# Attention sums with V as a 64-column stationary operand in two column tiles, bias and row maximum in one instruction

## What is computed

```python
def dilated_branch(q, k, v, rel_bias, window, dil):
    ...
    s = jnp.einsum("brnqhd,brnkhd->brnhqk", qb, kk) * (dh ** -0.5)
    ...
    s = s + bias.transpose(2, 0, 1)
    ...
    m = jnp.max(s, axis=-1, keepdims=True)
    p = jnp.exp(s - m)
    den = jnp.sum(p, axis=-1)
    o = jnp.einsum("brnqhk,brnkhd->brnqhd", p, vv) / den.transpose(0, 1, 2, 4, 3)[..., None]
    lse = (m[..., 0] + jnp.log(den)).transpose(0, 1, 2, 4, 3)
```

## Time and profile before

| | us |
|---|---|
| median of 3 runs (2899.11 to 2900.86) | 2900.39 |
| the profiled execution | 2887.13 |
| span of its trace | 2885.3 |
| attention, first to last matmul | 1396.5 to 1750.9 |

### The profile page before, as it was taken

One profiled execution on the slowest core, in us unless ns is written; L12 is line 12 of the kernel. 1 busy time (PEld: TensorE's weight loads), 2 busy tenths in 40 slices (PEclk: granted clock), 3 DMA queues, 4 the chain that ended last, 5 costly groups with the idle time before them and its releaser, 6 DMA issues. The chain is left out here.

```text
span 2885.3 us, 32536 instructions
## 1 busy us (share of the span) xinstructions
PE 2404.3 (83%) x9386; PEld 1351.9 (47%) x9387; DVE 1138.8 (39%) x1853; ACT 840.7 (29%) x1981; POOL 312.8 (11%) x298
## 2 busy tenths in 40 slices
PE   5779998898968999796799995999609999998940
PEld 2245554333424554685477773555404444444410
DVE  0122211666722263353478874565431111111126
ACT  3011111333223331121377784444101111111125
POOL 0000000000001110132113330000040000000022
PEclk9989999999988999898799997999859999999975
DMA  8631101111114664695222333444107756588778
GB/s 327 220 122 65 58 33 34 44 44 44 58 44 149 194 196 147 211 290 176 103 92 90 96 101 113 147 158 157 52 33 288 284 204 227 190 295 301 267 283 327
DMA packets 183271, 451.62 MB, mean 157 GB/s; under 512 B 42352, under 2 KB 78448, under 8 KB 169632
## 3 DMA queue, kind: packets, MB, share of 16 engines
q1 hardware_dynamic: 149200, 335.37, 34.3%
q10 hardware_dynamic: 21168, 72.36, 6.3%
q0 software_dynamic: 12832, 43.02, 4.3%
HBM read 321.22 MB, written 129.45 MB: 156 GB/s over the span
## 5 line engine op out<-in xcount | busy, mean ns | idle before, releaser
L1964 PE MATMUL ps<-ex_wgu,ex_xt 128*128 x800 | 355.3, 597 | 22.6 <-DMA ex_wgu<-in_w_gate_up 21.9
L418 PE MATMUL ps<-ht,pc_w 128*128 128x512 f32 x768 | 343.9, 610 | 33.9 <-ACT pc_pre L451 26.1
L334 PE MATMUL ps<-pt_wt,pt_ht 128*128 128x512 f32 (+1 forms) x768 | 250.7, 482 | 11.6 <-ACT pt_ht L344 11.5
L418 PEld LDWEIGHTS ps<-ht,pc_w 128*128 128x128 f32 x768 | 149.7, 196 | 227.3 <-issue 195.1
L1964 PEld LDWEIGHTS ps<-ex_wgu,ex_xt 128*128 128x128 f32 x800 | 148.9, 191 | 195.0 <-issue 195.0
L753 PE MATMUL ps<-ht,ci_w 128*128 128x512 f32 x512 | 224.5, 596 | 3.1 <-DMA ci_w<-in_w_chan 3.1
L1547 PE MATMUL ps<-w_out,mo_yt 128*128 128x512 f32 x512 | 224.4, 596 | 0.0
L334 PEld LDWEIGHTS ps<-pt_wt,pt_ht 128*128 128x128 f32 x768 | 127.0, 191 | 136.7 <-issue 123.0
L1360 PE MATMUL ps<-at_v,at_pt 128*128 128x128 f32 (+1 forms) x1200 | 184.0, 291 | 5.8 <-DMA at_v<-v_d 5.8
L1974 PE MATMUL ps<-ex_wd,ex_hidt 128*128 x400 | 181.8, 598 | 3.6 <-issue 2.2
L1422 ACT ACTIVATE at_p<-at_p,at_low 128x256 f32<-128x256 f32 (+1 forms) x384 | 174.0, 456 | 20.0 <-DVE at_low L1389 19.6
(11 more groups left out here) (288 smaller groups left out, 3112.6 us busy)
## 6 DMA issues: line engine op xcount, KB each, us to landing
ex_wgu<-in_w_gate_up SPq DMA_DIRECT2D x32, 2048.0 KB
ex_wd<-in_w_down SPq DMA_DIRECT2D x32, 1024.0 KB, 8.1
ys_d<-ex_y ACTq DMA_DIRECT2D x50, 512.0 KB
ada_w<-in_w_ada SPq DMA_DIRECT2D x12, 2048.0 KB, 8.5
at_v<-v_d SPq DMA_DIRECT2D x27, 512.0 KB, 4.0
o_d<-at_o SPq DMA_DIRECT2D x48, 264.0 KB
mo_o<-o_d SPq DMA_DIRECT2D x16, 792.0 KB, 8.8
ch_d<-pc_cv SPq DMA_DIRECT2D x12, 1024.0 KB, 3.9
```

Of the source, the lines that this page charges most:

```text
L334: last = nc.tensor.matmul(ps[:, bank, 0:hi - lo], ht[:, b, k, :], wt[:, k, lo:hi], start=(k == 0), stop=(k == KD - 1))
L418: last = nc.tensor.matmul(ps[:, g, :], w[:, b, k, :], m.ht[:, k, g * BANK:(g + 1) * BANK], start=(k == 0), stop=(k == KD - 1))
L1964: last = nc.tensor.matmul(ps[:, 2 + b, :], xt[:, b, k, :], wgu[:, bass.ds(half * WGU + k * 2 * DE, 2 * DE)], start=(k == 0), stop=(k == KD ...
```

## The change

The sums change roles. V, 64 columns of one head, becomes the stationary operand, and the transposed probabilities (128 columns) the moving one. The two heads of a step go to the two halves of the array's columns, and so to the two halves of the partitions of the result, which is now the sums transposed. At the end of a unit VectorE copies this (512 columns) to a new tile `ot`; TensorE turns it back with four transposes (`turn_o`, in the first step of the unit after next in the program's list, behind that step's `sums`); and VectorE copies it again into `o` in the second step (`take_o`). A last `turn_o` and `take_o` follow the last unit.

Scale, bias and maximum become one instruction for each head, `tensor_tensor_reduce`, which writes minus the scaled sum and its minimum. The bias table is multiplied by 8 to suit (one operation swapped for another in `bias_tables`), and `exp` gets a scale of -1. The copies of the transposed probabilities are shared: VectorE takes those of steps 1 and 3, ScalarE those of steps 0 and 2. The copy of `low` moves from VectorE to GpSimd, behind a wait for the last `exp` of the unit before.

```diff
@@ bias_tables
-                    nc.vector.tensor_tensor(rows[:, s], ps[0:AH, n, 0:BIAS_W], off[:, s], ALU.add).then_inc(*rows_ready.inc)
+                    nc.vector.scalar_tensor_tensor(rows[:, s], ps[0:AH, n, 0:BIAS_W], DH ** 0.5, off[:, s], ALU.mult, ALU.add).then_inc(*rows_ready.inc)
@@ attention
+        ot = R.sb("ot", [P, AW])
...
+        def take_pt(eng, copy, unit, s):
+            b, n, n2 = numbers(unit)
+            e, c, k = s % 2, n2 + s // 2, first_key(unit) // P
+            eng.wait_ge(*pt_done[e].n(c + 1))
+            eng.wait_ge(*pv_done[e].n(c))
+            copy(pt[:, e, :, k:, :], ps[:, 4 + e, :].rearrange("p (h k n) -> p h k n", h=2, k=2)[:, :, k:, :]).then_inc(*pt_ready[e].inc)
...
@@ SP
                         sp.wait_ge(*o_ready[b].n(n + 1))
+                        sp.wait_ge(*low_kept[b].n(n + 1))
@@ GpSimd, behind the gathers of q and k
+                    if prev:
+                        b, n, n2 = numbers(prev)
+
+                        pool.wait_ge(*p_ready[1].n(n2 + 2))
+                        pool.wait_ge(*out[b].n(n))
+                        pool.sem_inc(seen_pool, 1)
+                        nc.gpsimd.tensor_copy(o[:, b, AW:], low[:, b, :]).then_inc(*low_kept[b].inc)
@@ TensorE, sums
-                    for h in range(2):
-                        for k in range(k0, 2):
+                    for k in range(k0, 2):
+                        for h in range(2):
                             at = 2 * s + h
-                            w = slice(at * DH, min(at + 2, AH) * DH)
-                            last = nc.tensor.matmul(ps[:, 6 + b, w], pt[:, e, h, k, :], v[:, b, k, w], start=(k == k0), stop=(k == 1))
+                            last = nc.tensor.matmul(ps[h * DH:(h + 1) * DH, 6 + b, s * P:(s + 1) * P], v[:, b, k, at * DH:(at + 1) * DH], pt[:, e, h, k, :], start=(k == k0), stop=(k == 1))
                     last.then_inc(*pv_done[e].inc)
+                def turn_o(b, n):
+
+                    pe.wait_ge(*ot_ready[b].n(n))
+                    for s in range(STEPS):
+                        last = nc.tensor.transpose(ps[:, 6 + b, s * P:(s + 1) * P], ot[:, s * P:(s + 1) * P], m.ident)
+                    last.then_inc(*turned[b].inc)
...
                         if prev:
                             sums(prev, s)
+                        if s == 0 and earlier(unit, prev):
+                            turn_o(*earlier(unit, prev))
...
+                turn_o(numbers(prev)[0], UNITS // 2)
@@ VectorE
+                def take_o(b, n):
+                    dve.wait_ge(*turned[b].n(n))
+                    dve.wait_ge(*out[b].n(n - 1))
+                    nc.vector.tensor_copy(o[:, b, 0:AW], ps[:, 6 + b, :]).then_inc(*o_ready[b].inc)
+
                 for unit, prev in units(dve):
-                    if unit:
...
+                    for s in range(STEPS):
+                        if prev and s in (0, 2):
+                            take_pt(dve, nc.vector.tensor_copy, prev, s + 1)
+                        if unit:
...
+                            if s == 0:
+                                dve.wait_ge(*low_kept[b].n(n))
                             dve.wait_ge(*s_done[e].n(c + 1))
                             dve.wait_ge(*pt_done[e].n(c - 1))
-                            nc.vector.scalar_tensor_tensor(p[:, s, :, lo:], ps[:, 2 * e:2 * e + 2, lo:2 * P], DH ** -0.5, m.bias[:, unit[0][1], 2 * s:2 * s + 2, lo:], ALU.mult, ALU.add).then_inc(*s_read[e].inc)
-                            dve.wait_ge(*s_read[e].n(c + 1))
-                            nc.vector.tensor_reduce(low[:, b, 2 * s:2 * s + 2], p[:, s, :, lo:], AX.X, ALU.max, negate=True).then_inc(*max_ready[e].inc)
+                            dve.sem_inc(seen_dve, 1)
+                            for h in range(2):
+                                at = 2 * s + h
+                                nc.vector.tensor_tensor_reduce(p[:, s, h, lo:], ps[:, 2 * e + h, lo:2 * P], m.bias[:, unit[0][1], at, lo:], -(DH ** -0.5), BIG, ALU.add, ALU.min, stats(b, at)).then_inc(s_read[e].inc[0], 1)
+                        if s == 1 and earlier(unit, prev):
+                            take_o(*earlier(unit, prev))
                     if prev:
                         b, n, n2 = numbers(prev)
                         dve.wait_ge(*pv_done[1].n(n2 + 2))
-                        dve.wait_ge(*p_ready[1].n(n2 + 2))
-                        dve.wait_ge(*out[b].n(n))
-                        nc.vector.tensor_copy(o[:, b, AW:], low[:, b, :])
-                        nc.vector.tensor_copy(o[:, b, 0:AW], ps[:, 6 + b, :]).then_inc(*o_ready[b].inc)
+                        dve.wait_ge(*turned[1 - b].n(n + b))
+                        nc.vector.tensor_copy(ot[:, :], ps[:, 6 + b, :]).then_inc(*ot_ready[b].inc)
+                take_o(numbers(prev)[0], UNITS // 2)
@@ ScalarE
-                        if s >= 2 and unit:
-                            take_pt(unit, s - 2)
-                        elif s < 2 and prev:
-                            take_pt(prev, s + 2)
+                        if s == 3 and unit:
+                            take_pt(act, nc.scalar.copy, unit, 0)
+                        elif s == 1 and prev:
+                            take_pt(act, nc.scalar.copy, prev, 2)
...
-                                ins = nc.scalar.activation(p[:, s, h, lo:], p[:, s, h, lo:], ACT.Exp, bias=low[:, b, at:at + 1], accum_out=low[:, b, at + AH:at + AH + 1])
+                                ins = nc.scalar.activation(p[:, s, h, lo:], p[:, s, h, lo:], ACT.Exp, bias=low[:, b, at:at + 1], scale=-1.0, accum_out=low[:, b, at + AH:at + AH + 1])
```

More of the change, by code:

```diff
@@ L1270, in place @@
         return branch, BR[branch][0], first(i, j)
+    BIG = 3.0e38
     with Room(nc, "at") as R:
@@ L1284, in attention, with earlier @@
         q_ready, k_ready, o_ready = R.sigs("q_ready"), R.sigs("k_ready"), R.sigs("o_ready")
-        s_done, s_read, max_ready, p_ready = R.sigs("s_done", credit=3), R.sigs("s_read"), R.sigs("max_ready"), R.sigs("p_ready")
+        ot_ready, turned, low_kept = R.sigs("ot_ready"), R.sigs("turned"), R.sigs("low_kept")
+        seen_dve, seen_pool = R.plain("seen_dve"), R.plain("seen_pool")
+        s_done, s_read, p_ready = R.sigs("s_done", credit=3), R.sigs("s_read", step=2), R.sigs("p_ready")
         pt_done, pt_ready, pv_done = R.sigs("pt_done", credit=2), R.sigs("pt_ready"), R.sigs("pv_done", credit=3)
+        def earlier(unit, prev):
+            if unit:
+                b, n, _ = numbers(unit)
+                return None if isinstance(n, int) and n == 0 else (b, n)
+            return 1 - numbers(prev)[0], UNITS // 2
+        def take_pt(eng, copy, unit, s):
[4 more added lines that the diff above has]
+            copy(pt[:, e, :, k:, :], ps[:, 4 + e, :].rearrange("p (h k n) -> p h k n", h=2, k=2)[:, :, k:, :]).then_inc(*pt_ready[e].inc)
         with R.block() as block:
@@ L1373, in _, with stats @@
                             sums(prev, s)
+                        if s == 0 and earlier(unit, prev):
+                            turn_o(*earlier(unit, prev))
                     if not prev:
                         turn_p(unit, 0)
+                turn_o(numbers(prev)[0], UNITS // 2)
             @block.vector
             def _(dve):
-                for unit, prev in units(dve):
-                    if unit:
-                        b, n, n2 = numbers(unit)
-                        lo = first_key(unit)
-                        for s in range(STEPS):
+                def stats(b, at):
+                    return low[:, b, at:at + 1]
@@ new lines, in take_o @@
+                def take_o(b, n):
+                    dve.wait_ge(*turned[b].n(n))
+                    dve.wait_ge(*out[b].n(n - 1))
+                    nc.vector.tensor_copy(o[:, b, 0:AW], ps[:, 6 + b, :]).then_inc(*o_ready[b].inc)
+                for unit, prev in units(dve):
+                    for s in range(STEPS):
+                        if prev and s in (0, 2):
+                            take_pt(dve, nc.vector.tensor_copy, prev, s + 1)
+                        if unit:
+                            b, n, n2 = numbers(unit)
+                            lo = first_key(unit)
```

2 lines of the change are left out of this document (1 added, 1 removed).

## The result

The changed kernel is slower, by 1.7 to 2.3%: 2957.22 us median (2949.62 to 2963.15, 4 runs) against 2899.75 (2894.67 to 2900.86, 4 runs) of the kernel before, a ratio of 1.020 with a 95% interval of 1.0167 to 1.0233. The profiled execution took 2949.62 (span 2947.8), 62 more than that of the kernel before. Attention alone, from its first scores to the last of its sums, went from 354.1 to 406.8 us, so 53 of the difference lie there. Nearly all the rest lies ahead of it: attention starts 7.4 us later (at 1404.0), and the phase before it already starts 8.1 later (1378.9 against 1370.8). The same shows in e2_before_late_o, which alters nothing ahead of attention (1405.6), so I don't count it as the change's.

What follows compares the result with a forecast made beforehand. TensorE was taken to bound attention; full units -21.6 to -16.2 us, half units +2.5 to +6.7, end +1.5 and stalls +1 were taken as -12 from the 2900.4 median, giving 2888.5, range 2880 to 2936.

Steps and rivals of the forecast that it cites:

- the wait of SP: SP's extra wait for GpSimd's small copy, 2 to 3 us before the sums are there, costs nothing.
- the gain of the steps: TensorE's attention steps: 0.26 to 0.31 us saved per full step, 0.03 to 0.08 per half step, before turning back.
- slower: Outcome of a measurably slower kernel, resting on A, D and most of B and Rival E; chance 0.32.
- Rival E: Idle array time in half units drops attention's clock; each 20 us stretch costs about 9: 2898 to 2916; chance 0.06.
- A: Sums' column tiles run one behind the other, streams as long as today: +66 us, 2954; chance 0.12.
- B: Sums' column tiles run together but their loads don't hide: +20 to +45 us, 2908 to 2933; chance 0.11.
- third switch: A further change of array shape in each TensorE attention step, between sums and transposes, costing about 0.20 us.
- Turning back: Four transposes of the sums added to each unit on TensorE, without a further switch: 0.44 us.
- The end's 1.5 us: Attention's end: copy, four transposes and another copy after the last sums, 1.5 us more, not hidden.
- 1 us of stalls: Allowance for `turn_o` waiting on `ot` in half units, 0 to 0.3 us each; 1 us taken in all.
- C: `turn_o` waits for `ot`, or GpSimd's gathers come late, 0.1 to 0.3 us a unit: 2893 to 2903; chance 0.10.
- D: VectorE becomes the bound through a slower new instruction: +36 us, 2924; chance 0.07.

Runs made afterwards that it cites:

- e2_before_late_o: Kernel before, with only VectorE's copy of the 512 sums into o moved behind step 1 of the next unit; median 2948.65 us, ratio 1.0199.
- e1: Changed kernel with only SP's program altered: it stores the result of unit u-2 instead of u-1; median 2868.31 us, ratio 0.9901.
- e4: e1 with the sums' matmuls reordered in full units, both key blocks of one head first; median 2873.38 us, ratio 0.9927.
- e5: e1 with all copies of transposed probabilities on ScalarE, fused instruction kept on VectorE; median 2866.11 us, ratio 0.9908.
- e6: Changed kernel with the sums of before, no turning back, o copied at the unit's end; fusion and shared copies stay; median 2888.32 us, ratio 0.9978.
- e3: e1 with the fusion undone: scale and bias in one instruction, maximum in a second; copies stay shared; median 2893.55 us, ratio 0.9997.
- e8: e1 with the fusion undone and all copies of transposed probabilities on ScalarE; median 2873.39 us, ratio 0.9935.

## Why the prediction was wrong

I forecast 2888.5 (2880 to 2936), the median was 2957.2. Two terms failed: the wait of SP, put at nothing, and the gain of the steps, put too low. Point by point:

**SP's queue is the step that failed.** I wrote of SP's extra wait that it is for GpSimd's copy, "2 to 3 us before the sums are there. Cost nothing". Instead TensorE waited 54.7 us for V, 49 more than before. I looked at the wait that the diff adds and not at the one that it leaves in place: `o_ready` now comes half a unit or more later, and the next load of V is queued behind it. Its price could have been read from the trace of before: the store was issued right at the unit's end and the load 0.6 behind it, 3.6 us ahead of its sums, with a landing of 2.8, so there was 0.8 us to spare in a half unit. A delay of over two steps of 1.2 us had to break that. e2 shows that this alone makes 1.0199, e1 that its removal turns 1.020 into 0.9901. None of my rivals names this wait, so the 0.32 that I gave to "slower" stood on other causes.

**Rival E, the clock,** had the right effect and the wrong cause. I gave it 0.06 for the shapes. In e1, e4, e5 and e6 and in the kernel before the clock is at 1.00 (2.4 GHz) from attention's slow start (over by 1432) to its last sums, with old and with new shapes. The two kernels with waits for V show 0.50 (1.2 GHz): from 1697 to 1741 and again from about 1798 in the changed one, and for 27 us from 1777 in e2, besides short falls behind single pauses. In the changed kernel each fall began at a pause of 1.5 to 2.1 us or at most 1.5 us behind it. But it did not follow every such pause: eight of 1.35 to 1.74 us stand between 1745 and 1795, at 1.00 throughout. The shorter pauses in e3 and e8 (up to 1.0 us in e3 and 0.6 in e8) came with 1.00 throughout, behind the slow start. In the changed kernel five half units in a row took 8.7 us each, against 6.7 with the pause and 5.1 without. The runs of the changed kernel have a mean clock of 0.903 to 0.910 and are the longer the lower it is (2949.62 at 0.910, 2963.15 at 0.903). That the pauses bring the fall is what the pairs before and e2, and e1 and after, say: each differs in the pauses and not in the shapes. Why it fell where it did stays open.

**Rivals A and B** are out. The tiles work side by side, and their loads hide: pairs of matmuls over the same 128 rows start every 0.11 while the next loads run. The Trainium skill's rule ("TensorE: Matmul & The Clock Gate", Part 3) that loads overlap running matmuls only where the row group differs does not hold for column tiles here either: loads start at 1509.13, over the rows that the matmuls from 1508.97 on are using. The same part names loads into the background weight buffer as a second case, which the rule's wording leaves out; which of the two a load here is, no run shows.

**The cost of the steps** was right in kind and too dear in size. The third switch costs 0.15 rather than 0.20: the second pair starts 0.16 behind the first (the 64-column load, the lower of my two ends), and the first transposes gain from it too, 0.59 instead of 0.63 for the phase. Full step 1.81 (forecast 1.85 to 1.90), half step 1.16 (1.19 to 1.24), full unit 7.7 (7.9), half unit 5.1 (5.3). So half units lose nothing, where I had 2.5 to 6.7 us lost, and full units gain 0.9, 27 x 0.9 = 24. Turning back costs 0.49 where the switch stands ahead of it, and the following transposes get theirs back. The end's 1.5 us came out at 1.4. With the queue mended the change is worth 27 us of attention; I had 12. The 27 hold some 3 us of second-branch stalls that e6 loses too and that I had no term for. So with SP's term right I would still have missed: 0.9901 of 2899.75 is 2871, below my 2880. A slip stands in the sum as well: its terms with 1 us of stalls give -17 to -7, and -18 only without stalls.

**VectorE and rivals C and D.** The new instruction's rows, in half units of the changed kernel:

```profile
1775.72 0.28 DVE L1439 CUSTOM_DVE_ANT_0 at_p<-ps,bias 128x128 f32<-128x128 f32 x1
1775.93 0.08 DVE L1439 DVE_READ_ACCUMULATOR2_ANT at_low<- 128x1 f32 x1
1775.93 0.28 DVE L1439 CUSTOM_DVE_ANT_0 at_p<-ps,bias 128x128 f32<-128x128 f32 x1
1776.14 0.08 DVE L1439 DVE_READ_ACCUMULATOR2_ANT at_low<- 128x1 f32 x1
```

It takes 0.21 from start to start with 128 keys and 0.35 with 256, under my 0.29 to 0.39 and 0.42 to 0.52: the accumulator read starts together with the next instruction and adds nothing. With that much room on VectorE `turn_o` waited once in all, and D was far off. GpSimd was late only at attention's start (5.9 us, against 5.5 before), so C is out too. I was wrong that the fusion "is worth nothing" beyond its room: without it the gain falls from 29 us to 20 with all copies on ScalarE, and from 27 to 1 with the copies shared.

## What to carry to other kernels

When a change makes a result ready later, don't look only at who reads it: find each engine whose program waits for it, and what stands behind that wait, above all loads that the same engine issues, and compare the new issue time with the landing time and the slack that the trace of before shows. A pause in front of TensorE can cost more than its own length, because the granted clock may fall (49 us of pauses came with some 28 us lost to the clock here, by the estimate under e1), so a pause in a stretch that was covered deserves a higher price than its microseconds. And a part that is free by itself (the fusion) can be what another part (two more copies on the same engine) needs in order to be free.

## What the runs showed of the hardware

Two column tiles of 64 columns, over all 128 rows, take float32 matmuls side by side, whether the program alternates the tiles or not: eight records in 0.59 us from phase to phase, against 0.99 for eight over the whole array. The first two loads of 64 columns in a tile start 0.05 apart (1508.97 and 1509.02), later ones go every 0.11 with the matmuls, under which they hide. By my working from the rows, a switch of shape costs 0.20 us with a 128-column load behind it and 0.15 with a 64-column one or behind the column tiles. VectorE's accumulator read behind the fused instruction lasts 0.08 us and adds nothing from start to start, unlike ScalarE's, which takes 0.09.
